# VectorE adds an expert row's v part two dot products behind its own instead of one

## The chip, the cores and the metric

One Trainium2 chip, one core of it. The time is device microseconds (us) of one execution. The kernel before has a median of 3847.45 us over 3 runs (3844.36 to 3851.16). The profiled execution is a run of its own, of 3853.06 us.

## What is computed

Two layers of a decoder trunk over 512 tokens of width 1024, all in fp32. Each layer mixes differential attention, latent attention and a short convolution, and then adds a retrieval over 16384 experts of one neuron each (PEER). The change touches the sum of the retrieval alone:

```
expert = the 16 best of each of 8 heads            # 128 rows for every token
u_sel = u_tab[expert]
act = gelu(einsum('thkd,td->thk', u_sel, h))       # a dot product of 1024 with each row
w = gate * act
x += einsum('thk,thkd->td', w, v_tab[expert])      # a weighted sum of the rows' v parts
```

After it `x += sigmoid(rms(x) @ W_pg) * (p @ W_pp)`, and the next layer begins.

## The kernel before, in words

**Steps.** The 512 tokens of a layer are taken in halves of 256 (two tiles of 128 tokens, one token to a partition), so there are four pieces of work, d = 0 to 3. In step s the dense part of piece s+1 (norms, projections, attention, gates, queries, the choice of experts: the "stages") runs beside the expert rows of piece s. `stages_of` (L166) lists the stages of a step and `timeline` (L199) lays them out in PLAN. Step 3 has almost no stages left: after `ple_norm` and `ple_out` of piece 2 it is nothing but rows.

**Rows.** A "row" is one chosen expert for each of the 128 tokens of a tile: 128 gathered pieces of 8 KB (u and v side by side), 1 MB in all. A step has 256 rows, the run 1024. GpSimd gathers them with an indirect DMA (L505) into a ring of 8 slots (RING, L39), and waits in the order of the rows: before gather n it waits until row n-8 has been added (L499 to L504), on `pe_rows` or on `dve_rows`. With each row:

- VectorE forms the dot product of the u part with h (`dot`, L1166, operation L1171);
- ScalarE takes the gelu of it (L747), multiplies by the gate (L749) and, for a row that TensorE adds, makes a diagonal matrix of the weights (L755);
- the v part is added either by VectorE, with one scalar_tensor_tensor into x (`add_row`, L1174, operation L1180), or by TensorE, with four matmul instructions into PSUM (L1295). `shares` (L232) decides in advance which: 491 rows go to VectorE ("V" below), 533 to TensorE ("P"). Where TensorE is busy with weights (qkv, convolutions, gates, out) all rows are V, in the norms and in topk all are P, elsewhere they are mixed, and in the last step they alternate V P V P.

**The order on each engine.** Before each stage every engine serves the same number of rows from PLAN. On VectorE `serve` (L1192) issues the dots and adds of a batch, and then the stage's own operations follow. VectorE keeps the V rows whose add is still to come in the list `waiting`. Before the change it issues, after each dot, the add of the row waiting there, which is the row of the dot before. A list that isn't empty at the end of a batch is carried into the next batch, behind the next stage's first dot. On ScalarE `serve` (L742) treats the rows of the batch, in order, before the stage's own work, so ScalarE enters a stage only once VectorE has formed the last dot of that batch; and a weight is late when ScalarE is held in the stage before. Gelu, exp, sigmoid and square root need different function tables, so that a table load (L747 or L535, ACT_TABLE_LOAD) often stands ahead of them.

**Stages of which the prediction speaks**, each with the VectorE operation that follows its batch: `diff_flip` (L901, from L905), `conv_c` (nothing on VectorE; ScalarE evacuates its matmuls, L584), `diff_sub` (L913, from L917; it waits for `evacs` of the attention output), `mla_norm` (L928; ScalarE begins with squares, L634), `mla_up` (L646, evacuations on ScalarE), `mla_sums` (L944, from L951; it waits for those evacuations), `mla_qk` (L968; ScalarE takes a square root first), `mla_rope` (L980), `mla_scores` (L1015), `x_norm` and `ffn_norm` (L798; ScalarE forms the sums of squares first, L538), `query` and `rank` (L1051, from L1059; it waits for the evacuated scores). At the end of each tile of 128 rows `add_sum` (L1183) adds what TensorE summed in PSUM, having first emptied `waiting` up to that row.

Of the kernel before, what the change touches and what calls it, by code (L numbers as in the profile page):

```python
# [279 lines left out]
def trunk(nc, a):  # L280
    ctx = ExitStack()
    with ctx:
# [488 lines left out]
        def _(dve):  # L771
# [381 lines left out]
            waiting = []  # L1153
# [12 lines left out]
            def dot(row):  # L1166
                dve.wait_ge(landed[row.slot], 16 * (row.lap + 1))
                if row.j == 0:
                    dve.wait_ge(h_ready, row.tiles_before + 1)
                u = ring[:, row.slot, 0:D]  # L1170
                dve.scalar_tensor_tensor(u, u, 1.0, h_ffn[:, row.tile, :], ALU.mult, ALU.mult,  # L1171
                                         accum_out=dots[:, row.j:row.j + 1]).then_inc(dots_ready, 1)

            def add_row():  # L1174
                row = waiting.pop(0)
                xs = x[:, 2 * (row.step % 2) + row.tile, :]
                dve.wait_ge(weight_ready, row.number + 1)
                if row.dve_before:
                    dve.wait_ge(dve_rows, row.dve_before)
                dve.scalar_tensor_tensor(xs, ring[:, row.slot, D:2 * D], weight[:, row.j:row.j + 1], xs, ALU.mult, ALU.add)\  # L1180
                    .then_inc(dve_rows, 1)

            def add_sum():  # L1183
                row = ended.pop(0)
                while waiting and waiting[0].number <= row.number:
                    add_row()
                xs = x[:, 2 * (row.step % 2) + row.tile, :]
                dve.wait_ge(pe_rows, PE_BEFORE[row.number + 1])
                dve.wait_ge(dve_rows, row.number + 1 - PE_BEFORE[row.number + 1])
                dve.tensor_tensor(xs, ps_sum[:, :, :].rearrange("p b n -> p (b n)"), xs, ALU.add).then_inc(sum_added, 1)  # L1190

            def serve(n, last=False):  # L1192
                if n and ended:
                    add_sum()
                for row in rows.take(n):
                    dot(row)
                    if waiting:
                        add_row()
                    if not row.by_pe:
                        waiting.append(row)  # L1200
                    if last and ended and row.j == 2:
                        add_sum()
                    if row.last:
                        ended.append(row)
                if last:
                    while waiting:
                        add_row()
                    while ended:
                        add_sum()
# [26 lines left out]
            for step, row, rest in PLAN:  # L1236
                with_rows = 0 <= step < STEPS
                if with_rows:
                    make_h(step)
                for (name, d, *more), at, units in row:  # L1240
                    assert (n_bank, n_op) == (at.taken, at.dve), (name, d, more, n_bank, n_op, at.taken, at.dve)
                    serve(units)
                    stage[name](at, d, *more)
                if with_rows:
                    serve(rest, True)
# [465 lines left out]
```

## Time and profile before

| | |
|---|---|
| Median of 3 runs | 3847.45 us |
| Profiled execution: its own time / span | 3853.06 / 3851.2 us |
| Busy: TensorE, VectorE, ScalarE, GpSimd | 76%, 67%, 39%, 35% of the span |
| Mean granted TensorE clock | 0.886 |
| Moved by DMA | 1298.67 MB, 1073.81 MB of it gathers |
| The chain that ended last, by engine | TensorE 46%, VectorE 20%, DMA 16%, ScalarE 12%, issue 5% |

How to read it: times are us from the span's start unless marked ns. PE is TensorE, DVE is VectorE, ACT is ScalarE, POOL is GpSimd. `L1180` is line 1180 of the kernel. "a<-b" names what is written and what is read. "[1.33 <-ACT weight L749]" behind an instruction is the time that its engine sat idle before it, and who ended that wait. The chain is followed back from the last instruction, at each step to what released it or to the instruction before it on its engine; only what lies on it sets the end. Idle time of an engine that is not on it costs nothing.

### The profile page before, as it was taken

How to read it: one execution, taken by the hardware profiler on the slowest of the kernel's cores; microseconds unless marked ns; L12 is line 12 of the kernel's file. 1: busy time of each engine (PE TensorE's matmuls, PEld its weight loads, DVE VectorE, ACT ScalarE, POOL GpSimd, SP SyncE). 2: the span in 40 equal slices, each digit the busy share in tenths (PEclk: the TensorE clock that was granted, in tenths of full speed). 3: DMA queues.
4: the chain of work that ended last, by engine and by line, in shares of the span. 5: the costliest groups of instructions: out<-in, count | busy, mean ns of one | idle time of the engine just before them, and what ended most of it. 6: DMA issues, size and time to landing. Idle time of an engine off the chain costs nothing.

```text
span 3851.2 us, 28862 instructions
## 1 busy us (share of the span) xinstructions
PE 2941.2 (76%) x8156; PEld 1500.1 (39%) x8156; DVE 2586.3 (67%) x5236; ACT 1487.1 (39%) x4001; POOL 1354.1 (35%) x1033
## 2 busy tenths in 40 slices
PE   7689848777998788766988778777998786555556
PEld 4444614534446333523436334534446332111112
DVE  1321486786657976776667976776667987777773
ACT  2220224448433334448433344448533343222222
POOL 0000033243433443334432533243333345555651
PEclk9879978888999898989999898889999897777777
DMA  4224379899998999999998999889999999999994
GB/s 149 71 75 150 120 289 366 300 368 354 394 378 357 385 369 380 363 367 374 401 382 348 384 384 375 308 358 361 379 375 361 387 384 415 422 421 421 422 421 171
DMA packets 182400, 1298.67 MB, mean 337 GB/s; under 512 B 20320, under 2 KB 21856, under 8 KB 26592
## 3 DMA queue, kind: packets, MB, share of 16 engines
q0 software_dynamic: 147456, 1073.81, 69.5%
q1 hardware_dynamic: 34784, 223.01, 14.8%
q8 instruction: 66, 1.08, 0.1%
q14 instruction: 94, 0.77, 0.1%
HBM read 1294.64 MB, written 2.10 MB: 337 GB/s over the span
## 4 chain that ended last, share of the span: by engine, by line
PE 46%; DVE 20%; DMA 16%; ACT 12%; issue 5%; POOL 1%; SPq 0%; DVEq 0%; ACTq 0%; POOLq 0%
DMA ring<-in_uv,experts 12%; PE ps_sum L1295 12%; PE ps_act L1529 8%; PE ps_act L1357 8%; PE ps_act L1402 7%; DVE ring L1171 6%; DMA wt<-in_weights 3%; PE ps_dve L1357 3%; PE ps_dve L1557 2%; DVE x L1180 2%; ACT L747 2%; PE ps_dve L1402 2%; ACT L535 2%; ACT diag L755 1%; ACT area_e L535 1%
## 5 line engine op out<-in xcount | busy, mean ns | idle before, releaser
L505 POOL DMA_INDIRECT ring<-in_uv,experts x1024 | 1351.6, 1320 | 2423.3 <-PE ps_sum L1295 936.4
L1295 PE MATMUL ps_sum<-ring,diag 128*128 128x512 f32 x2132 | 1240.5, 727 | 707.8 <-ACT diag L755 688.3
L1171 DVE SCALAR_TENSOR_TENSOR ring<-ring,h_ffn 128x1024 f32<-128x1024 f32 x1024 | 1231.7, 1221 | 174.1 <-DMA ring<-in_uv,experts 167.6
L1295 PEld LDWEIGHTS ps_sum<-ring,diag 128*128 128x128 f32 x2132 | 447.5, 224 | 1382.6 <-ACT diag L755 949.6
L1180 DVE SCALAR_TENSOR_TENSOR x<-ring,weight,x 128x1024 f32<-128x1024 f32 x491 | 630.0, 1283 | 205.2 <-ACT weight L749 204.4
L747 ACT ACTIVATE dots<-dots 128x1 f32<-128x1 f32 x1024 | 206.7, 202 | 1363.9 <-DVE ring L1171 1362.3
L1402 PE MATMUL ps_act<-area_h,wt 128*128 128x256 f32 x1536 | 347.0, 385 | 2.6 <-ACT area_h L521 2.6
L1529 PE MATMUL ps_act<-wt,area_h 128*128 128x512 f32 x768 | 339.9, 598 | 9.6 <-DMA wt<-in_weights 9.5
L1357 PE MATMUL ps_act<-wt,area_h 128*128 128x512 f32 (+1 forms) x768 | 336.1, 598 | 5.1 <-ACT area_h L521 5.0
L749 ACT ACTIVATE weight<-dots,gate 128x1 f32<-128x1 f32 x1024 | 304.1, 297 | 33.3
L1402 PEld LDWEIGHTS ps_act<-area_h,wt 128*128 128x128 f32 x1536 | 295.1, 194 | 54.1 <-issue 10.8
L521 ACT ACTIVATE area_b<-ps_act 128x256 f32<-128x256 f32 (+2 forms) x240 | 100.0, 431 | 379.2 <-PE ps_act L1402 166.6
L1529 PEld LDWEIGHTS ps_act<-wt,area_h 128*128 128x128 f32 x768 | 145.4, 191 | 197.9 <-issue 176.7
L1357 PEld LDWEIGHTS ps_act<-wt,area_h 128*128 128x128 f32 x768 | 150.3, 197 | 185.3 <-issue 177.7
L755 ACT ACTIVATE diag<-ident,weight 128x128 f32<-128x128 f32 x533 | 215.1, 404 | 17.3
L747 ACT ACT_TABLE_LOAD x143 | 183.5, 1283 | 2.5
L1557 PE MATMUL ps_dve<-wt,area_t 128*128 128x512 f32 x384 | 168.7, 592 | 0.0
L1341 PE MATMUL ps_act<-ident,area_b 128*128 128x128 f32 (+1 forms) x448 | 84.2, 337 | 86.0 <-DVE area_b L812 38.8
L535 ACT ACT_TABLE_LOAD x107 | 137.3, 1283 | 1.9
L1036 DVE TENSOR_TENSOR area_b<-ps_dve,area_b 128x512 f32<-128x512 f32 x32 | 22.1, 692 | 148.8 <-PE ps_dve L1557 148.8
L1357 PE MATMUL ps_dve<-wt,area_b 128*128 128x512 f32 x256 | 110.9, 594 | 1.9 <-ACT area_b L521 1.9
L1557 PEld LDWEIGHTS ps_dve<-wt,area_t 128*128 128x128 f32 x384 | 73.0, 190 | 91.8 <-issue 91.8
(176 smaller groups left out, 2155.7 us busy)
## 6 DMA issues: line engine op xcount, KB each, us to landing
wt<-in_weights SPq DMA_DIRECT2D x192, 1024.0 KB
ring<-in_uv,experts POOLq DMA_INDIRECT x1024
wt<-in_weights SPq DMA_DIRECT2D x12, 512.0 KB
wt<-in_weights SPq DMA_DIRECT2D x4, 768.0 KB
x<-in_x SPq DMA_DIRECT2D x4, 512.0 KB, 5.2
area_y<-in_keys SPq DMA_DIRECT2D x4, 512.0 KB, 9.3
area_f<-in_keys SPq DMA_DIRECT2D x4, 512.0 KB, 10.0
area_f<-in_ffn_rows SPq DMA_DIRECT2D x4, 512.0 KB, 3.8
```

The lines of the kernel that those rows point to most:

```text
L505: pool.indirect_dma_start(ring[:, row.slot, :], None, a[f"uv{row.step // 2}"][:, :], bass.IndirectOffsetOnAxis(ap=experts[:, row.step % 2, ...
L535: act.activation(*args, **kw).then_inc(act_ops, 1)
L747: act.activation(dots[:, j], dots[:, j], ACT.Gelu).then_inc(gelu_ready, 1)
L749: act.activation(weight[:, j], dots[:, j], ACT.Copy, scale=gate[:, row.step % 2, row.tile, j])\
L755: act.activation(diag[:, row.pe_before % DIAGS, :], ident[:, :], ACT.Copy, scale=weight[:, j])\
L1171: dve.scalar_tensor_tensor(u, u, 1.0, h_ffn[:, row.tile, :], ALU.mult, ALU.mult, accum_out=dots[:, row.j:row.j + 1]).then_inc(dots_ready, 1)
L1180: dve.scalar_tensor_tensor(xs, ring[:, row.slot, D:2 * D], weight[:, row.j:row.j + 1], xs, ALU.mult, ALU.add)\
L1295: ins = pe.matmul(ps_sum[:, b, :], diag[:, row.pe_before % DIAGS, :], ring[:, row.slot, D + b * 512:D + (b + 1) * 512], start=row.pe_first ...
L1357: ins = pe.matmul(banks[t][:, 0:width], lhsT[:, 4 * kh + k, t * P:(t + 1) * P], w[:, k, 0:width], start=(kh + k == 0), stop=(kh == 1 and k ...
L1402: ins = pe.matmul(b[:, 0:HALF], w[:, k, c * P:(c + 1) * P], hT[:, k, :], start=(k == 0), stop=(k == KT - 1))
L1529: ins = pe.matmul(bank, hT[:, 4 * kh + k, t * P:(t + 1) * P], w[:, k, :], start=(kh + k == 0), stop=(kh == 1 and k == 3))
L1557: ins = pe.matmul(b, (ydT, ymT, ycT)[br][:, k, t * P:(t + 1) * P], w[:, k, :], start=(k == 0), stop=(k == 3))
```

## The change

After the dot of row r VectorE now adds the first waiting row only if its number is below r - 1. A V row r is so added behind dot r+2 instead of behind dot r+1, and up to two rows wait.

```diff
@@ -1194,7 +1194,7 @@
                     add_sum()
                 for row in rows.take(n):
                     dot(row)
-                    if waiting:
+                    if waiting and waiting[0].number < row.number - 1:
                         add_row()
                     if not row.by_pe:
                         waiting.append(row)
```

## Rows read from the trace of the kernel before

**Rows 1.** Stretches: length; busy PE, PEld, DVE, ACT, POOL; clock, DMA share, GB/s.

```profile
515.00:1394.00 879.00, 709.50 (x2090) 377.93 (x2090) 655.74 (x1369) 392.48 (x1011) 338.08 (x261) 0.91 0.93 368
1394.00:2256.00 862.00, 691.29 (x1930) 354.70 (x1930) 634.14 (x1308) 387.96 (x1019) 331.22 (x256) 0.92 0.94 374
2256.00:3138.00 882.00, 716.92 (x2142) 382.74 (x2142) 648.79 (x1307) 400.76 (x1020) 322.46 (x256) 0.92 0.92 366
...
3200.00:3790.00 590.00, 340.34 (x473) 106.41 (x472) 431.15 (x589) 165.02 (x587) 330.72 (x231) 0.75 1.01 418
```

**Rows 2.** Waits of the whole span: who, for whom, us in total, times, longest.

```profile
POOL ring L505 <- DVE x L1180: 912.6, 390, 12.1
...
DVE x L1180 <- ACT weight L749: 204.4, 82, 8.2
...
DVE ring L1171 <- DMA ring<-in_uv,experts: 167.6, 132, 2.5
```

**Rows 3.** The same wait for gathers, in the stretch 3200 to 3790.

```profile
DVE ring L1171 <- DMA ring<-in_uv,experts: 151.4, 118, 2.5
```

**Rows 4.** VectorE in time order: first and last of 14 waits on the chain.

```profile
789.07 1.28 DVE L1180 SCALAR_TENSOR_TENSOR x<-ring,weight,x 128x1024 f32<-128x1024 f32 x1 [2.77 <-ACT weight L749]
...
2936.96 1.28 DVE L1180 SCALAR_TENSOR_TENSOR x<-ring,weight,x 128x1024 f32<-128x1024 f32 x1 [7.66 <-ACT weight L749]
2938.16 0.87 DVE L1059 MAX8 area_t<-area_e 128x8 f32<-128x128 f32 x4
```

**Rows 5.** ScalarE in time order, ahead of the last of them.

```profile
2935.75 0.75 ACT L521 ACTIVATE area_e<-ps_act 128x256 f32<-128x256 f32 x2 [1.86 <-PE ps_act L1589]
```

**Rows 6.** Chain at `diff_sub`: start us, us, what.

```profile
1645.71 0.34 ACT area_y L521 x2
...
1647.69 0.69 DVE scratch L917
```

**Rows 7.** ScalarE, then VectorE, in time order at `mla_up`.

```profile
1672.14 1.28 ACT L747 ACT_TABLE_LOAD   x1
...
1674.00 1.28 DVE L1180 SCALAR_TENSOR_TENSOR x<-ring,weight,x 128x1024 f32<-128x1024 f32 x1 [1.33 <-ACT weight L749]
```

**Rows 8.** VectorE in time order at `mla_sums`.

```profile
1690.48 1.28 DVE L1180 SCALAR_TENSOR_TENSOR x<-ring,weight,x 128x1024 f32<-128x1024 f32 x1 [7.13 <-ACT weight L749]
1691.69 1.22 DVE L1171 SCALAR_TENSOR_TENSOR ring<-ring,h_ffn 128x1024 f32<-128x1024 f32 x1
...
1692.83 1.75 DVE L951 TENSOR_TENSOR area_e<-area_b 128x1536 f32<-128x1536 f32 x1
```

**Rows 9.** Chain at `mla_norm`.

```profile
2540.71 1.20 DVE x L1180
...
2543.09 0.21 ACT dots L747
```

**Rows 10.** Chain at `ffn_norm`.

```profile
2014.32 1.20 DVE x L1180
2015.51 4.59 DVE ring L1171 x8
...
2020.13 0.21 ACT dots L747
```

**Rows 11.** Chain at `diff_flip`.

```profile
2475.76 1.14 DVE ring L1171 x2
2476.90 0.09 DVE soft L905
```

**Rows 12.** Chain: a gather under light load, and one in the last step.

```profile
510.29 5.75 DMA ring<-in_uv,experts
...
3454.89 15.03 DMA ring<-in_uv,experts
```

**Rows 13.** VectorE in time order, in the last step.

```profile
3452.54 1.23 DVE L1171 SCALAR_TENSOR_TENSOR ring<-ring,h_ffn 128x1024 f32<-128x1024 f32 x1
...
3455.03 1.23 DVE L1171 SCALAR_TENSOR_TENSOR ring<-ring,h_ffn 128x1024 f32<-128x1024 f32 x1 [1.25 <-DMA ring<-in_uv,experts]
```

## The prediction, made before the change was built or run

> **What bounds the kernel now.** I read the stretches first, one per step [rows 1]. Steps 0 to 2 take 879, 862 and 882 us and no engine is full in them: TensorE is busy for 80%, VectorE for 74%, the DMA for 92 to 94%. The last step is another thing: 590 us with the DMA at its ceiling (1.01, 418 GB/s). Then the waits [rows 2]: VectorE waits for a row's weight 82 times, 204.4 us in all, and this is what the change aims at. It waits for gathers 167.6 us, of which 151.4 lie in the last step [rows 3], so before it gathers arrive early (16 us in 2600). GpSimd waits 912.6 us for VectorE's adds before it gathers again: the ring is always full, and an add that comes later is a gather that starts later.
>
> Last the chain, read from end to end. All 82 waits for weights lie before 3200 us, where the last step's pure row stretch begins. Of them only 14 are on the chain, the first at 789.07 and the last at 2936.96 [rows 4], together 2.8+0.4+1.3+4.6+2.2+3.6+1.3+7.1+2.2+3.3+1.3+6.6+0.3+7.7 = 44.6 us. The other 160 us lie beside TensorE's matmuls.
>
> **The change, part by part.** Nothing is added or removed: 491 adds stay 491. Each moves back by one dot. Write d for a dot (1.15 us from start to start) and a for an add (1.20, [rows 8, 9]). Only the place of the adds in a batch matters, in two ways: how many stand before the batch's *last dot* (ScalarE waits for that dot before it enters the stage) and how many stand in the batch *at all* (VectorE's stage operations follow it). I wrote out each batch of PLAN that lies on the chain in both orders and took the difference by how the chain leaves the batch, to ScalarE or to VectorE. Letters are the rows' dots.
>
> Gains:
> - `diff_sub`, three times (V P a becomes V P). The add waits for its weight while the stage's L917 has its input since 1645.71 + 0.34 = 1646.05 and starts at 1647.69 [rows 6]. The add moves into the next batch: 1.6 us each, 4.8.
> - `mla_norm`, three times (P a P V P a P becomes P P a V P P a, in step 0 likewise). The chain leaves by the last dot to ScalarE [rows 9]: one add less before it, 3 x 1.2 = 3.6.
> - `mla_up`, three times. After the square root's table ScalarE loads gelu's (1.28 us), and the add is 1.33 us late [rows 7]. Moved behind one more dot it is on time, since 1.15 of that dot and the dot before cover it: 3 x 1.33 = 4.0.
> - `mla_sums` (P V P a P becomes P a V P P a). The weight is late by 7.13 us because ScalarE is held by the evacuations before it [rows 8]. One more dot doesn't cover that: the add still waits, but the last dot now stands in the wait instead of behind it, 1.15 us in steps 1 and 2. In step 0 the add leaves the batch, 1.7. Together 4.0. The stall itself stays at about 6 us.
> - `mla_qk`: an add less before the last dot in steps 1 and 2, one more in step 0: 1.2.
> - `conv_c` (V a V a V becomes V V a V), three times: 3.6.
> - `rank`, once a step. The scores are evacuated at 2935.75 + 0.75 = 2936.50 [rows 5], yet L1059 starts at 2938.16, behind the late add [rows 4]: 1.7 each, 5.1.
>
> Sum 26.3 us.
>
> Costs, where an add that used to lie in VectorE's idle time is carried into a batch on the chain:
> - `ffn_norm`, three times (P a P P P P becomes P a P a P P P): its batch follows a stretch of V rows, so two adds are carried in instead of one, both before the last dot for which ScalarE waits [rows 10]: 3.6. `x_norm` the same where the chain passes through all of it, once: 1.2.
> - `diff_flip` (a lone dot becomes d a) with L905 straight behind it [rows 11], twice a step: 7.2.
> - `mla_rope` and one `mla_scores` of step 0: 2.4.
> - `query` and `rank` batches where V P a becomes V a P, with ScalarE next, three times: 3.6.
>
> Sum 18.0. Pairs that cancel in neighbouring batches (`mla_pv` and `mla_scores`, `scores` and `rank`) are left out. Topk has only P rows and `ple_out` only V rows before and behind: zero.
>
> Net in steps 0 to 2: 18.0 - 26.3 = -8.3 us.
>
> **GpSimd's queue and the last step.** A V row's slot comes free one d and one a later, 2.35 us, and every gather behind it in GpSimd's order too. In steps 0 to 2 the early arrival of gathers covers it (above); if that cover were gone, each place would cost up to 2.35. In the last step a row lands every 3455.03 - 3452.54 = 2.49 us [rows 13], so 8 slots last 19.9 us, and a gather takes about 15 [rows 12], nearly all of it queueing, for under light load it takes 5.75 [rows 12]. Now 15/2.49 = 6 gathers are in flight. The add of V row r moves from behind dot r+1 to behind dot r+2, 2.49 us later: about 5 in flight. The 5.75 us need only 5.75/2.49 = 2.3, so the transfers stay full. Nor is a dot delayed: d + a = 2.35 fits in 2.49. What can be lost is the entry into this step, where slots from `ple_out`'s V rows come free 2.35 us later while the DMA isn't yet full: between 0 and 2.4, I take 1.2. The last two rows are V P, with the add behind the last dot in either order: zero.
>
> Total -8.3 + 1.2 = -7.1 us on 3853.06, the profiled execution's own time, which is 5.6 above the median; on the median 3840.4, told as 3841.
>
> A rule against any gain: the Trainium skill (DMA: Bandwidth & Descriptors, "Where 436 GB/s comes from") says that about 358 GB/s of HBM per core binds such loads. By it steps 0 to 2 would be bound by transfers and the change worth nothing. The trace disagrees: 418 GB/s [rows 1].
>
> **Rivals.**
> - *The waits are worth more.* Near-critical paths carry the other 160 us, and costs that I charge to VectorE are swallowed by TensorE's waits. With all gains and no costs 26 us: 3821. For it: 204.4 us is the largest wait of VectorE [rows 2]. Against: 68 of the 82 lie beside matmuls. 15%.
> - *The transfers set the pace.* Steps 0 to 2 move 366 to 374 GB/s with 92 to 94% of the DMA busy; a shorter chain would only meet gathers and weights later in the queue. Nothing gained: 3847. Against: 418 GB/s are possible, and there are 16 us of gather waits. 14%.
> - *The slots come free too late, and it is slower.* The place is where a batch of V rows is followed by rows consumed fast: before topk in each step and at the entry of the last. The price is a row's 2.4 us at each of four places, 10 us if the gains too are eaten: 3857. It decides once VectorE's waits for gathers before 3200 us grow from 16 us by more than the 7 gained. In the last step it would take over fully only if more than 5 gathers were needed in flight, which 5.75 us of latency speaks against. 16%.
>
> **How the numbers follow.** My forecast has 55%, with a range of its own of -15 to 0 us. This kernel's measurement can tell about 0.2%, 7.7 us, from no change, and the forecast lies just short of it: I split it 22 faster to 33 same. With the rivals, faster 22 + 15 = 37%, same 33 + 14 = 47%, slower 16%. The range runs from the first rival's 3821, less 1 for its size, to the third's 3857.
>
> **What would show it.** VectorE's wait for weights should fall from 204.4 to under 100 us, mostly to longer waits (`mla_sums`, at about 6 us each); `mla_up`'s 1.33 us and `diff_sub`'s should be gone. VectorE's waits for TensorE and for evacuated data should grow by nearly as much, since 160 us lay beside those. A `ffn_norm` batch should show two adds before its last dot. Gathers in the last step should take about 12.5 us instead of 15 at the same 2.49 us per row and 418 GB/s; steps 0 to 2 should be shorter by 0 to 5 us each. I am wrong if a step changes by over 10 us, if gather waits before 3200 us grow past 25 us, or if a row of the last step takes over 2.55 us.

## The result and the profile after

| | before | after |
|---|---|---|
| Median | 3851.16 us (3844.36 to 3862.60, 7 runs) | 3866.95 us (3859.39 to 3870.34, 7 runs) |
| Ratio, with its 95% interval | | 1.0038 (1.0021 to 1.0055) |
| Profiled execution: its own time / span | 3853.06 / 3851.2 | 3870.34 / 3868.5 |
| Mean granted TensorE clock | 0.886 | 0.880 |

The change makes the kernel 15.8 us slower by the medians, and by the ratio's interval 8 to 21 us. The forecast was 7 us faster, in a range that ended at 3857 us. From the first dot of a step to the first dot of the next, the profiled executions take 878.7, 862.0 and 881.9 us before and 879.4, 869.2 and 890.8 after; the last step, to its last dot, takes 652.1 and 654.0. So nearly all of the loss lies in steps 1 and 2.

The stretches of the profile after, with the columns of [rows 1]:

```profile
515.00:1394.00 879.00, 706.73 (x2090) 376.18 (x2090) 653.50 (x1367) 390.01 (x1011) 334.99 (x262) 0.91 0.92 367
1394.00:2256.00 862.00, 692.82 (x1917) 356.68 (x1918) 631.72 (x1304) 382.31 (x1014) 330.98 (x253) 0.91 0.93 372
2256.00:3138.00 882.00, 717.79 (x2134) 383.12 (x2133) 640.57 (x1296) 394.90 (x1010) 324.17 (x254) 0.91 0.92 363
3200.00:3790.00 590.00, 347.52 (x476) 109.87 (x474) 433.46 (x591) 165.95 (x587) 316.45 (x234) 0.74 1.01 420
```

The averages hide nearly everything. VectorE gets through 2, 4 and 11 instructions fewer in the first three windows, in the same time, and the DMA moves 1 to 3 GB/s less; the last step moves 420 GB/s against 418. What changed is seen in the waits, here those of the whole span (who, for whom, us in total, times, longest):

```profile
POOL ring L505 <- DVE x L1180: 1303.0, 456, 14.4
...
POOL ring L505 <- PE ps_sum L1295: 553.5, 268, 16.8
...
DVE ring L1171 <- DMA ring<-in_uv,experts: 190.8, 155, 3.0
```

and one of them before:

```profile
POOL ring L505 <- PE ps_sum L1295: 936.4, 417, 16.7
```

GpSimd waits 1303.0 us for VectorE's adds, against 912.6 [rows 2]. Most of this is the same waiting under another name: its waits for TensorE's rows fell from 936.4 to 553.5 us, and the two together went from 1849.0 to 1856.5. Ahead of 3200 us VectorE's waits for ScalarE and for the DMA are, in the profile after,

```profile
DVE x L1180 <- ACT weight L749: 78.3, 30, 7.1
...
DVE ring L1171 <- DMA ring<-in_uv,experts: 36.1, 34, 2.2
```

and the second of them before the change, over the same stretch,

```profile
DVE ring L1171 <- DMA ring<-in_uv,experts: 14.0, 13, 2.1
```

So the change did what it was said to do: the waits for late weights fell from 204.4 us (82) to 78.3 (30). The waits for gathers ahead of 3200 us grew by 22 us. In the stretch 3200 to 3790 the wait for gathers is as it was [rows 3]:

```profile
DVE ring L1171 <- DMA ring<-in_uv,experts: 149.4, 116, 3.0
```

**Where the 16 us arise.** Every kernel here serves the same 1024 rows in the same order, so the start of the dot of a given row can be compared between traces. The table gives, for the first dot of some batches, how much later it starts than in the profiled execution before, each kernel counted from its own first dot. (That first dot itself starts up to 6.5 us earlier or 4.4 later from one execution to the next, ahead of any row, which is why it is taken out.) The columns to the right of "after" are experiments told below (slots late is 1, mla late 2, dense late 4, no add in flip 5, seven slots 10 less 9, last late 3). The last column is a check on the others: up to the last step its kernel is the kernel before.

| Batch (step) | before, us | after | slots late | mla late | dense late | after, no add in flip | after - before, 7 slots | last late |
|---|---|---|---|---|---|---|---|---|
| conv_b (0) | 728.8 | -0.2 | 0.0 | -1.3 | +0.3 | -2.7 | -0.4 | -0.2 |
| taps (0) | 759.7 | +1.0 | 0.0 | -0.8 | +1.3 | -3.8 | +0.8 | -0.2 |
| mla_turn (0) | 861.8 | -0.5 | +0.1 | -2.7 | +0.7 | -4.9 | +0.2 | -0.3 |
| gate_a (0) | 981.3 | +2.3 | +3.2 | -0.4 | +3.0 | -7.3 | +2.4 | 0.0 |
| query (0) | 1166.8 | +4.5 | +4.6 | +0.1 | +4.6 | -5.5 | +3.1 | +0.1 |
| x_norm (1) | 1447.8 | +0.5 | +0.6 | -0.4 | +0.4 | -9.6 | +0.5 | -3.4 |
| conv_b (1) | 1591.9 | +3.5 | +0.9 | -0.4 | +0.3 | -8.8 | +5.8 | -3.6 |
| taps (1) | 1617.2 | +7.6 | +0.7 | -0.4 | +4.4 | -7.6 | +10.1 | -3.6 |
| mla_turn (1) | 1722.9 | +4.0 | +0.6 | -3.0 | +3.8 | -9.4 | +10.0 | -3.5 |
| query (1) | 2026.5 | +5.1 | +3.5 | 0.0 | +6.3 | -8.9 | +7.1 | -3.0 |
| query, 5th (1) | 2078.2 | +7.8 | +3.4 | 0.0 | +8.6 | -8.9 | +7.7 | -3.0 |
| x_norm (2) | 2309.0 | +8.9 | +2.2 | 0.0 | +9.0 | -11.4 | +6.5 | -4.7 |
| conv_b (2) | 2462.5 | +10.2 | +3.4 | -0.4 | +10.3 | -10.7 | +10.0 | -3.8 |
| taps (2) | 2494.4 | +13.5 | +3.4 | -0.4 | +13.7 | -10.4 | +13.4 | -3.7 |
| mla_turn (2) | 2600.5 | +10.5 | +3.5 | -3.2 | +13.4 | -12.6 | +11.5 | -3.7 |
| topk (2) | 3024.9 | +11.0 | +3.2 | -2.3 | +11.4 | -9.0 | +12.7 | -4.0 |
| topk, 2nd tile (2) | 3078.8 | +15.5 | +6.7 | -1.8 | +12.4 | -3.9 | +16.9 | -3.5 |
| last step, 33rd row | 3232.2 | +18.9 | +7.5 | -1.0 | +13.9 | -2.1 | +19.6 | +0.7 |
| last row | 3790.8 | +18.8 | +7.5 | -0.9 | +13.5 | -1.9 | +18.0 | -0.9 |

These are single executions, and they differ where nothing was changed. Kernel 3 starts rows up to 5 us earlier than the kernel before while it is still the same kernel, and 3.5 of these appear between query (0) and x_norm (1), where the changed kernel too wins 4.0: there it was the profiled execution before that was slow (its granted clock from 1380 to 1450 us is 0.88, that of kernel 3 0.94). Kernel 6, told below, is the kernel before up to a probe in step 0, and ahead of it, at conv_b (0), it is 6.5 us early, with a granted clock of 0.90 against 0.87 from 520 to 730 us; it ran on another chip than kernel 3. The sum of a long stretch is therefore no better than some 5 us. A short piece is: from conv_b to taps, kernels 1, 2 and 3 differ from the kernel before by at most 0.2 us in steps 1 and 2, and 0.5 in step 0.

Read down the column "after": 4.1 and 3.3 us are lost between conv_b and taps in steps 1 and 2, where the `diff_flip` batches lie; 3.6 and 3.0 are won back by `mla_turn`, where I had forecast gains; 2.7 are lost inside the queries of step 1; 4.5 within the last topk and 3.4 more up to the 33rd row of the last step. From there on nothing is added.

**The place between conv_b and taps**, step 1. Before the change, VectorE and then TensorE in order of time:

```profile
1602.80 1.22 DVE L1171 SCALAR_TENSOR_TENSOR ring<-ring,h_ffn 128x1024 f32<-128x1024 f32 x1
...
1603.94 0.16 DVE L905 RECIPROCAL soft<-soft 128x2 f32<-128x2 f32 x1
...
1605.19 0.44 PE L1445 MATMUL ps_act<-ident,area_e 128*128 128x128 f32 x2 [1.28 <-DVE area_e L911]
...
1605.68 7.07 PE L1402 MATMUL ps_act<-area_h,wt 128*128 128x256 f32 x32
```

and after it:

```profile
1607.15 1.22 DVE L1171 SCALAR_TENSOR_TENSOR ring<-ring,h_ffn 128x1024 f32<-128x1024 f32 x1
...
1608.29 1.28 DVE L1180 SCALAR_TENSOR_TENSOR x<-ring,weight,x 128x1024 f32<-128x1024 f32 x1
1609.49 0.16 DVE L905 RECIPROCAL soft<-soft 128x2 f32<-128x2 f32 x1
...
1610.74 0.44 PE L1445 MATMUL ps_act<-ident,area_e 128*128 128x128 f32 x2 [2.50 <-DVE area_e L911]
...
1611.24 8.76 PE L1402 MATMUL ps_act<-area_h,wt 128*128 128x256 f32 x32
```

An add carried in from an earlier batch stands between the dot and the reciprocal, and everything behind it is 1.2 us later. By the order of rows that PLAN and `shares` give, the change puts one add more between conv_b and taps in step 0 (in the sixth flip) and two in steps 1 and 2 (in the fifth and the sixth; this is the fifth). TensorE sits idle for 2.50 us instead of 1.28. Then its next 32 matmuls, the same ones, take 8.76 us instead of 7.07. The two stretches tell why (columns of [rows 1], the granted clock is the third number from the end), first before, then after:

```profile
1605.00:1613.00 8.00, 7.81 (x38) 6.70 (x40) 7.16 (x10) 3.00 (x11) 3.56 (x4) 1.00 1.00 410
```

```profile
1611.00:1620.00 9.00, 9.00 (x38) 7.38 (x36) 5.51 (x8) 1.93 (x7) 3.68 (x3) 0.81 1.03 388
```

TensorE had its full 2.4 GHz before, and after the longer idle it ran part of the run at 1.2 GHz. Two adds of 1.2 us and 1.7 us of clock are the 4.1 us of step 1; with 1.0 us of clock (8.4 us for these matmuls, against 7.4) they are 3.4 in step 2, where the table has 3.3. In the queries of step 1 a run of matmuls is longer too, by 2.5 of the 2.7 us lost there; on the chain before,

```profile
2030.19 14.08 PE ps_act L1402 x64
```

and after,

```profile
2036.44 16.57 PE ps_act L1402 x64
```

**The gains and what came for them.** At `diff_sub` the add is gone from in front of L917, at `mla_sums` it is no longer 7.13 us late [rows 8]. VectorE after, in order of time (step 1):

```profile
1654.18 0.69 DVE L917 TENSOR_TENSOR scratch<-area_y 128x512 f32<-128x512 f32 x1 [2.83 <-ACT area_y L521]
...
1680.86 1.29 DVE L1180 SCALAR_TENSOR_TENSOR x<-ring,weight,x 128x1024 f32<-128x1024 f32 x1 [0.86 <-ACT weight L749]
...
1685.45 1.23 DVE L1171 SCALAR_TENSOR_TENSOR ring<-ring,h_ffn 128x1024 f32<-128x1024 f32 x1 [1.01 <-DMA ring<-in_uv,experts]
...
1690.42 1.23 DVE L1171 SCALAR_TENSOR_TENSOR ring<-ring,h_ffn 128x1024 f32<-128x1024 f32 x1 [1.25 <-DMA ring<-in_uv,experts]
...
1692.88 1.22 DVE L1171 SCALAR_TENSOR_TENSOR ring<-ring,h_ffn 128x1024 f32<-128x1024 f32 x1 [1.22 <-DMA ring<-in_uv,experts]
...
1695.09 1.28 DVE L1180 SCALAR_TENSOR_TENSOR x<-ring,weight,x 128x1024 f32<-128x1024 f32 x1 [0.99 <-ACT weight L749]
1696.30 1.75 DVE L951 TENSOR_TENSOR area_e<-area_b 128x1536 f32<-128x1536 f32 x1
```

L917 starts 6.49 us later than before (1647.69, [rows 6]) and L951 3.47 later (1692.83, [rows 8]), so 3.0 us are won between them. The add at 1695.09 waits only 0.99 us for its weight, where the forecast had some 6, partly because the dots ahead of it wait 1.01, 1.25 and 1.22 us for gathers. Before, no dot waited for a gather between 1640 and 1834; after, 5.9 us are spent so.

**The last topk** after, VectorE in order of time; before, there is one wait of 0.3 us in this stretch:

```profile
3046.29 1.23 DVE L1171 SCALAR_TENSOR_TENSOR ring<-ring,h_ffn 128x1024 f32<-128x1024 f32 x1 [1.25 <-DMA ring<-in_uv,experts]
...
3052.57 1.23 DVE L1171 SCALAR_TENSOR_TENSOR ring<-ring,h_ffn 128x1024 f32<-128x1024 f32 x1 [0.40 <-DMA ring<-in_uv,experts]
...
3055.05 1.23 DVE L1171 SCALAR_TENSOR_TENSOR ring<-ring,h_ffn 128x1024 f32<-128x1024 f32 x1 [1.24 <-DMA ring<-in_uv,experts]
```

**The last step** is much as forecast; the chain after:

```profile
3435.15 12.18 DMA ring<-in_uv,experts
...
3448.59 1.21 DVE x L1180
...
3450.05 12.17 DMA ring<-in_uv,experts
```

A gather takes 12.2 us instead of 15.03 [rows 12], as it does in experiment 3, where only this step was changed, and the rows come at the same pace: from the last step's 33rd row to its last row 558.5 us after, 558.6 before.

### The profile page after: what moved, and what is told of

Read it like the earlier page. It is cut to its first block, busy times and chain, and to the rows that moved or that the text cites. A ratio compares the mean times of both kernels' runs of the same rounds, so it can differ in the third digit from the quotient of the medians.

```text
span 3868.5 us, 28862 instructions
## 1 busy us (share of the span) xinstructions
PE 2959.6 (77%) x8156; PEld 1510.8 (39%) x8156; DVE 2585.7 (67%) x5236; ACT 1477.7 (38%) x4001; POOL 1341.6 (35%) x1033
## 4 chain that ended last, share of the span: by engine, by line
PE 45%; DVE 20%; DMA 19%; ACT 11%; issue 5%; POOL 0%; SPq 0%; DVEq 0%; ACTq 0%; POOLq 0%
DMA ring<-in_uv,experts 15%; PE ps_sum L1295 10%; PE ps_act L1402 8%; PE ps_act L1529 8%; PE ps_act L1357 7%; DVE ring L1171 6%; DMA wt<-in_weights 3%; DVE x L1180 3%; PE ps_dve L1357 3%; PE ps_dve L1557 2%; ACT L747 2%; PE ps_dve L1402 2%; ACT area_e L535 1%; ACT L535 1%; ACT diag L755 1%
## 5 line engine op out<-in xcount | busy, mean ns | idle before, releaser
L505 POOL DMA_INDIRECT ring<-in_uv,experts x1024 | 1339.1, 1308 | 2456.2 <-DVE x L1180 1303.0
L1295 PE MATMUL ps_sum<-ring,diag 128*128 128x512 f32 x2132 | 1255.1, 734 | 696.8 <-ACT diag L755 683.2
L1180 DVE SCALAR_TENSOR_TENSOR x<-ring,weight,x 128x1024 f32<-128x1024 f32 x491 | 629.2, 1281 | 78.4 <-ACT weight L749 78.3
L1529 PE MATMUL ps_act<-wt,area_h 128*128 128x512 f32 x768 | 339.7, 597 | 10.4 <-DMA wt<-in_weights 10.4
L1020 DVE CUSTOM_DVE_ANT_0 area_e<-ps_dve,mask 128x128 f32<-128x128 f32 (+3 forms) x64 | 31.4, 490 | 133.7 <-PE ps_dve L1428 72.7
```

Of the source, the lines that this page charges most:

```text
L505: pool.indirect_dma_start(ring[:, row.slot, :], None, a[f"uv{row.step // 2}"][:, :], bass.IndirectOffsetOnAxis(ap=experts[:, row.step % 2, ...
L1295: ins = pe.matmul(ps_sum[:, b, :], diag[:, row.pe_before % DIAGS, :], ring[:, row.slot, D + b * 512:D + (b + 1) * 512], start=row.pe_first ...
L1529: ins = pe.matmul(bank, hT[:, 4 * kh + k, t * P:(t + 1) * P], w[:, k, :], start=(kh + k == 0), stop=(kh == 1 and k == 3))
```

## The experiments

Ten kernels ran, each timed against the kernel before beside it on the same chip, in five rounds: 1 to 4 on one chip, 5 to 7 on a second, 8 to 10 on a third. The table sets all traces against the one profile before. Theory A: the loss comes from ring slots that come free a row later, so that gathers come late. Theory B: it comes from adds carried into batches on the chain, with what TensorE's clock makes of them.

### 1. The slots alone

The adds keep their place, but GpSimd gathers into a V row's slot only once the dot two behind has been formed.

```diff
                         pool.wait_ge(dve_rows, former.dve_before + 1)
+                        pool.wait_ge(dots_ready, former.number + 3)
```

> The adds stand where they stood before, behind the next dot; only GpSimd waits longer for a VectorE row's slot, until the dot of row r+2 has been formed. The slots are so late by about one dot, 1.2 us less than in the changed kernel, and nothing moves on VectorE. Theory A (the slots come free too late, gathers arrive late in the lower-slack places): 8 to 16 us slower than the kernel before, VectorE's waits for gathers before 3200 us grow from 16 us to 30 or more. Theory B (the adds moved onto VectorE's path cost the time): within 3 us of the kernel before, waits for weights at 204 us, waits for gathers under 20 us.

Measured: 3859.0 us against 3851.56, ratio 1.0015 (1.0001 to 1.0029), so 6 us slower (0.4 to 11). Its waits for gathers ahead of 3200 us:

```profile
DVE ring L1172 <- DMA ring<-in_uv,experts: 19.6, 22, 2.1
```

The time lies between the two expectations; the waits for gathers, under 20 us, are as theory B had them. The slots are a part of the loss, by this run not the whole. But a slot is later here by one dot only (1.15 us), in the changed kernel by a dot and an add (2.35), so 6 us is what half the lateness costs, and this run sets no upper bound. In the table its last topk costs 3.5 us and the entry into the last step 0.8, the same place as in the changed kernel. The waits grew by 5.6 us only, so the 36.1 us of the changed kernel are not explained by this half: its slots are later still, and its dots come in another rhythm.

### 2. Two behind only in the latent attention

Here, in 3 and in 4 `serve` is told whether to hold back; the difference is the condition.

```diff
-                    if waiting:
+                    if waiting and (not late or waiting[0].number < row.number - 1):
                         add_row()
...
-                    serve(units)
+                    serve(units, late=name in ("diff_sub", "mla_norm", "mla_up", "mla_sums", "mla_qk"))
```

> Two dots behind only in the batches of diff_sub, mla_norm, mla_up, mla_sums and mla_qk, where the two traces side by side show the changed kernel gaining 4 to 5 us a step; elsewhere as before. Theory A: the gain of the order is there, but the slots are late in just those stages, which wait for gathers: a net of 0 to 6 us faster. Theory B: all of the three steps' gains and none of the costs, 10 to 14 us faster than before.

Measured: 3845.31 us, ratio 0.9975 (0.9961 to 0.9989), 10 us faster by the ratio (4 to 15) and 6 by the medians. Waits for gathers ahead of 3200 us are 27.8 us. The gains are real, and here alone they make a faster kernel. The trace shows 1.9, 2.6 and 2.8 us won from taps to `mla_turn` in the three steps, and most of that lost again by the next gate. The span of this one execution, 3846.0, is 5.2 below before, which agrees with the medians and lies inside the interval; the trace does not show where more would arise.

### 3. Two behind only in the last step

```diff
-                    serve(units)
+                    serve(units, late=step == STEPS - 1)
...
-                    serve(rest, True)
+                    serve(rest, True, late=step == STEPS - 1)
```

> Two dots behind only in the last step. Both theories: steps 0 to 2 unchanged, the entry into the pure row stretch 2.3 us later (what the two traces show side by side) and the same 2.49 us a row after it: 1 to 3 us slower. If the fewer gathers in flight cost rate, it would be 10 us or more.

Measured: 3851.24 us, ratio 0.9993 (0.9979 to 1.0006), 8 us faster to 2 slower. The forecast 1 to 3 us are neither seen nor excluded, a loss of 10 is. The last step can do with one gather less in flight.

### 4. Two behind from `x_norm` to `diff_pv`

```diff
-                    serve(units)
+                    serve(units, late=name in ("x_norm", "qkv", "latent", "conv_c", "conv_x", "conv_b", "taps", "diff_sq", "diff_norm", "diff_turn", "diff_scores", "diff_flip", "diff_pv"))
```

> Two dots behind only from x_norm to latent (norm, qkv, convolutions, scores of the differential attention), the part in which the changed kernel loses 5 to 6 us a step. Theory A: gathers arrive 10 us and more ahead of their use here, so the loss is small here by itself, and shows where the later slots meet the mla stages: waits for gathers near 1640 to 1700 us, 3 to 8 us slower in all. Theory B: the adds carried into diff_flip and x_norm cost their 1.2 us each: 8 to 15 us slower, with no waits for gathers.

Measured: 3863.24 us, ratio 1.0027 (1.0010 to 1.0045), 10 us slower (4 to 17). This is some two thirds of the loss, without longer waits for gathers than before (13.4 us ahead of 3200, against 14.0). The table puts 4.1 and 3.4 us of it between conv_b and taps, and 2.3 into the queries of step 1, as in the changed kernel. Theory B holds for what is lost here. It need not be two thirds of the changed kernel's loss, for the parts do not add up: experiments 1 and 4 lose 16 us together and experiment 2 wins 10, which leaves some 7 of 16.

### 5. The changed kernel, with no add issued in a `diff_flip` batch

```diff
-                    if waiting and waiting[0].number < row.number - 1:
+                    while name != "diff_flip" and waiting and waiting[0].number < row.number - 1:
                         add_row()
...
-                    serve(units)
+                    serve(units, name=name)
```

> The changed kernel, but in the batches of diff_flip no add is issued at all; the held adds follow the next dot of another stage. If the adds carried into diff_flip are what costs in steps 0 to 2 (1.2 us each on the chain, and 1.7 us more where TensorE, idle 2.5 instead of 1.3 us, then runs the next 32 convolution matmuls in 8.6 instead of 6.9 us), the loss of 4 us between conv_b and taps of steps 1 and 2 goes and the whole is 5 to 10 us faster than the changed kernel, so about 5 to 10 us slower than the kernel before. If the late slots are all of the loss, it is as slow as the changed kernel, 13 to 18 us slower than before, or slower still, for slots come free later yet.

Measured: 3856.57 us against 3850.68, ratio 1.0014 (1.0002 to 1.0026), 5.5 us slower than before (1 to 10). About 10 of the 16 us went with a few adds; the two intervals leave 1 to 17 for it, all on the faster side. From conv_b to taps it now takes 1.1 us less, 1.2 more and 0.3 more than before, instead of 1.2, 4.1 and 3.3 more. The last topk is still 5.1 us longer. What stays is not accounted for: the loss of experiment 1 less the gain of experiment 2 would be 4 us faster than before. Its own column cannot tell, for this profiled execution wins 2.7 us ahead of conv_b (0), and all three kernels run on the second chip do so (2.7, 6.5 and 6.0 us), the probe's too, where nothing was changed there. Slots that are later than in experiment 1 may be the rest; no run shows it.

### 6. A probe in place of the add

The kernel before, with one reduction of 1024 elements, read by nobody, ahead of the reciprocal in the fifth `diff_flip` in each of steps 0 to 2 (its lines lie up to five lower).

```diff
+                if d and i == 4:
+                    dve.tensor_reduce(junk[:, :], h_ffn[:, 0, :], AX, ALU.add).then_inc(probed, 1)
+                    dve.wait_ge(probed, d)
                 dve.wait_ge(act_ops, WHERE[("diff_scores", d, i)].act + 2)
```

> The kernel before with one more operation of VectorE, a sum over 1024 elements of about 1.2 us, ahead of the reciprocal of diff_flip 4 in each of steps 0 to 2. No row's add moves and no slot comes free later. If an operation carried into this place costs its own time alone: 1.2 us a step, 3.6 in all. If TensorE's longer idle time also brings it to the lower clock: 2.9 us in steps 1 and 2, the 32 matmuls behind it 8.6 us instead of 6.9 and the granted clock of that stretch 0.8 instead of 1.0. If it lies beside other work: nothing.

Measured: 3853.6 us, ratio 1.0006 (0.9995 to 1.0018), 2 us, which the timing does not resolve. The trace does; VectorE, TensorE and the stretch in step 1:

```profile
1599.89 1.21 DVE L907 TENSOR_REDUCE junk<-h_ffn 128x1 f32<-128x1024 f32 x1
1601.14 0.17 DVE L910 RECIPROCAL soft<-soft 128x2 f32<-128x2 f32 x1
...
1602.39 0.44 PE L1450 MATMUL ps_act<-ident,area_e 128*128 128x128 f32 x2 [2.54 <-DVE area_e L916]
...
1602.89 8.76 PE L1407 MATMUL ps_act<-area_h,wt 128*128 128x256 f32 x32
```

```profile
1603.00:1611.00 8.00, 8.00 (x31) 6.74 (x30) 6.36 (x9) 1.80 (x7) 3.80 (x3) 0.79 1.01 415
```

A different instruction of the same length, with the rows' order untouched, gives the same idle (2.54 against 2.50 us), the same lower clock and the same 8.76 us. It is thus the 1.2 us on VectorE that does it, not the order of the adds or the ring. From conv_b to taps the probe costs 2.1, 3.0 and 2.2 us in steps 0, 1 and 2: 1.2 of its own, and 0.8, 1.7 and 1.0 in the 32 matmuls behind it (8.8, 8.8 and 8.4 us, against 8.0, 7.1 and 7.4 before). Over all kernels this run of 32 matmuls in steps 1 and 2, and the 64 of the query in step 1, took (us):

| | flip, step 1 | flip, step 2 | query, step 1 |
|---|---|---|---|
| before, and kernels 1, 2, 3, 5, 7, 8 and 9 | 7.1 | 7.4 | 14.1 |
| after | 8.8 | 8.4 | 16.6 |
| kernel 4 | 8.8 | 8.4 | 16.0 |
| kernels 6 and 10 | 8.8 | 8.4 | 14.1 |

In the two flips the split has no exception. In step 1 it goes with the idle time of TensorE ahead of the run: 1.28 or 1.29 us in the eight kernels of the first line, 2.50 in kernels after, 4 and 10, 2.54 in 6. In the query it shows in two of the four only, and kernel 4 has no add moved there, so that one depends on more than the flip.

### 7. Experiments 2 and 5 together

```diff
-                    if waiting:
+                    back = name in ("diff_sub", "mla_norm", "mla_up", "mla_sums", "mla_qk")
+                    while name != "diff_flip" and waiting and waiting[0].number < row.number - back:
                         add_row()
```

> Two dots behind only from diff_sub to mla_qk, as in the second experiment, one dot behind elsewhere, and no add in the batches of diff_flip. It takes the gain of the second experiment (9.6 us) and takes the adds away from where they cost. If both are right: 12 to 18 us faster than before. If late slots undo it: no better than the second experiment, and more waits for gathers than its 28 us before 3200 us.

Measured: 3843.75 us, ratio 0.9981 (0.9967 to 0.9994), 7 us faster than before, and no better than experiment 2, whose interval overlaps. The expectation was too high. It counted adds in the flips of the kernel before as dear, which experiment 8 tests. But this kernel also waits 34.0 us for gathers ahead of 3200, against 27.8 in experiment 2, and that is what the other branch of the expectation, late slots, had named; the two are not told apart.

### 8. The kernel before, with no add in a `diff_flip` batch

```diff
-                    if waiting:
+                    while name != "diff_flip" and waiting:
                         add_row()
```

> The kernel before, in which VectorE issues no add of a v part in the batches of diff_flip; they are done with the next dot product outside. Theory: before the change these batches hold few adds ahead of their two-part reciprocal and scaling, and the dear ones came only with the change, by adds carried in from earlier batches. Then this kernel lies within 4 us of before (3847 to 3855 where before is 3851). Rival: any add in these batches costs its 1.2 us and the fall of TensorE's clock, before as after, and the gain of the fifth run over the changed kernel was only that. Then it is 7 to 10 us faster.

Measured: 3850.8 us against 3849.76, ratio 0.9990 (0.9972 to 1.0007), a ratio that leaves out one of the twelve executions, which took 7080.72 us and whose cause is not known. Nothing that can be measured is to be had there before the change: the dear adds came with it. That fits experiment 7.

### 9 and 10. Both kernels with seven slots

```diff
-RING = 8
+RING = 7
```

> The kernel before with seven ring slots instead of eight. Both theories: slower than before, gather waits ahead of 3200 us over 30 us where before has 14; it is the base for the next run. Size: every gather that is issued early is issued one row later, 10 to 40 us slower.

> The changed kernel with seven ring slots instead of eight, to be set against the kernel before with seven. Theory that slots that come free a row later are part of the loss: with one slot less every such row counts, and the changed kernel is 22 to 35 us slower than its base, more than the 15.8 us with eight slots; its gather waits ahead of 3200 us lie over 60 us. Rival, that the loss is the carried adds alone: 12 to 18 us slower than its base, as with eight slots.

Measured: 3884.59 us (1.0078, 1.0049 to 1.0107) and 3910.99 us (1.0151, 1.0122 to 1.0179). The changed kernel is now 26.4 us slower than its base (six runs each, which spread over 17 and 16 us, so that some 7 us either way are left open), against 15.8 with eight slots. The waits for gathers ahead of 3200 us are, in this order,

```profile
DVE ring L1171 <- DMA ring<-in_uv,experts: 64.4, 48, 8.0
```

```profile
DVE ring L1171 <- DMA ring<-in_uv,experts: 98.7, 69, 12.1
```

The difference of the waits grew from 22 to 34 us, and the timing points the way of theory A. It doesn't prove it: the profiled executions differ by 25.3 us in their own times, but 9.4 of these lie ahead of the first dot, and from there to the last row it is 18.0, much as with eight slots (18.8; the column "7 slots" of the table). What the pair does show is that the slots are scarce: one fewer costs the kernel before 0.8%, 30 us by the ratio and 35 by the medians.

## Why the prediction was wrong

**What held.** The waits for weights fell below 100 us (78.3). The last step kept its 2.5 us per row, with gathers of 12.2 us, as worked out from 5 gathers in flight. Experiment 2 shows that the gains in the latent attention exist. The sign that I had named for being wrong, gather waits ahead of 3200 us over 25 us, came: 36.1.

**The cover of the gathers.** "In steps 0 to 2 the early arrival of gathers covers it" is the first step that failed. I read it from 16 us of waits in 2600, an average. The slack is small in some places: ahead of `mla_sums` and in the last topk a row later meant waiting at once. Experiment 1 gives this term 6 us for half the lateness; I had 1.2. The third rival named the place (topk, the entry of the last step) and the mechanism; its price of four times 2.4 us was wrongly spread, as the topks of steps 0 and 1 lost nothing and the last one alone lost 3.5 (experiment 1) to 4.5 us.

**The flips.** The term was 7.2 us, a carried add of 1.2 six times. The trace has 1.2 + 4.1 + 3.3 = 8.6 us between conv_b and taps. The sum is near, the working is not. By the kernel's order of rows eight flips take up an add, not six: three of them, the second of each step, lie ahead of conv_b, and five between conv_b and taps, 1 + 2 + 2, which is 6.0 us. The other 2.7 us are TensorE's clock: 8.76 - 7.07 = 1.7 in step 1 and 8.4 - 7.4 = 1.0 in step 2, behind the add of the fifth flip. In step 0 that flip serves no rows, no add falls into it, and its 32 matmuls take 8.0 us before and after. With 16.57 - 14.08 = 2.5 us in the query, the clock took some 5 us that no term had. The prediction costed each wait by its own length and did not ask what TensorE's idling does to the work behind it.

**The gains that did not come.** `rank` was to give 1.7 us a step. The add is indeed gone from in front of L1059, yet from the first query to topk nothing is won: +4.5 to +4.6 in step 0, +11.1 to +11.0 in step 2. The chain before did run through the add, but a second path of the same length lay beside it: ScalarE's weight and diagonal, on which TensorE waits before its next 32 matmuls. Before, then after:

```profile
2939.66 7.07 PE L1402 MATMUL ps_act<-area_h,wt 128*128 128x256 f32 x32
```

```profile
2948.53 0.87 DVE L1059 MAX8 area_t<-area_e 128x8 f32<-128x128 f32 x4 [8.38 <-ACT area_e L521]
...
2951.64 7.07 PE L1402 MATMUL ps_act<-area_h,wt 128*128 128x256 f32 x32
```

L1059 comes 10.4 us later than before (2938.16, [rows 4]) and the matmuls 12.0, as late as everything ahead of them; the 1.6 us won on VectorE end in idle time. `conv_c`, 3.6 us, was read from its first batch alone. In the kernel's order the second one goes the other way, V V a becomes V a V, with an add more before its last dot, and the two cancel. `diff_sub` was read so too: the add that leaves its first batch stands in the second (P V becomes P a V), which was not among the costs. The second L917 starts at 1652.68 before and at 1661.28 after, 8.6 us later where the first is 6.5 later. From taps to `mla_turn` the terms gave 4.8 + 3.6 + 4.0 + 4.0 + 1.2 - 2.4 = 15.2; the trace has 1.5 + 3.6 + 3.0 = 8.1, and experiment 2, with the new order in these batches up to `mla_qk` alone, has 7.3. This is the largest term that was mis-sized.

**Costs that did not come.** `query` and `rank`, 3.6 us, are not seen. `ffn_norm` was near: 3.6 expected, and from `mix_turn`, the batch ahead of it, to the first query the changed kernel loses 0.9, 0.7 and 1.1 us.

Against the -7.1 us of the prediction that makes 7.1 (attention) + 5.1 (`rank`) + 3.6 (`conv_c`) + 1.4 (flips) + 2.5 (clock in the query) + 4.6 (slots) - 3.6 (`query` and `rank`) - 0.9 (`ffn_norm`) = 19.8 more, or +12.7; measured was +15.8. The match is in part luck: most of the terms are read from one execution, the column they are read from scatters by some 5 us, and the slots are in it at half their lateness.

**The rule weighed in the prediction.** Of the 358 GB/s of HBM per core (the Trainium skill, DMA: Bandwidth & Descriptors, "Where 436 GB/s comes from") the traces after say what those before did: 420 GB/s over the last step. That transfers set the pace of steps 0 to 2 is not what the runs show: experiment 2 moves the same bytes in less time, and the changed kernel takes longer at 1 to 3 GB/s less.

**Open.** Why the changed kernel loses 3.0 us from `x_norm` to conv_b in step 1 where experiment 4, with the same adds, loses nothing. Why the changed kernel and kernels 1, 2 and 4 lose 2.3 to 3.1 us from `mla_turn` to `gate_a` in step 0, where kernel 3 loses 0.3; kernel 4 has no add moved there. What the slots cost at their full lateness, and what is left in experiment 5. Whether the lower clock in the query follows from the flip, or only from how the two happen to fall: a kernel that keeps TensorE busy through the carried add was not tried.

## What to carry to other kernels

A deferred operation does not vanish: list the batches into which it is carried, and look first for those with a short chain from engine to engine behind them, where it costs its length and, if TensorE waits for it, also the matmuls behind at a lower clock. Defer it where the wait is (five stages: 6 to 10 us faster) and not everywhere (16 us slower). And read the slack of a prefetch at its smallest place, not from the total of its waits.

## What was not expected of the hardware

- A run of 32 fp32 matmuls of 128x256 took 7.07 us after TensorE had been idle for 1.28 us, and 8.76 us after 2.50 or 2.54, at a granted clock of 1.00 against 0.81 and 0.79. In all twelve executions, on three chips at least, this run went by the idle time ahead of it (1.28 or 1.29 us in eight, 2.50 or 2.54 in four). Near this point 1.2 us on another engine cost 2.9.
- A like run of 32 matmuls in the prologue, at 122 to 128 us, ahead of any row and any changed instruction, took 7.1 us in the executions of before and of kernels 1, 2 and 9, and 8.8 in those of after and of kernels 3 to 8 and 10. So the granted clock also varies from one execution to the next by itself, and a single trace can't price it over a long stretch: where nothing was changed, two executions came to differ by up to 6.5 us.
- One slot of eight fewer for gathers of 1 MB cost the kernel before 35 us by the medians (3884.59 against 3849.76) and 30 by the ratio. One gather fewer in flight in the last step, at 420 GB/s, cost nothing that the timing of experiment 3 resolves.
